# Squares of the RMS norms folded by VectorE before TensorE's column sums, and the order of transposes and value products in the attention rounds, on one core

## What is computed

```
for i in range(4):                                  # layers
    h = rms_norm(x, g[0])
    m = retention(h) | causal pooling(h) | dilated attention(h)   # i mod 3
    x = x + rms_norm(m, g[1])
    x = x + rms_norm(swiglu(rms_norm(x, g[2])), g[3])
rms_norm(x, g) = x * rsqrt(mean(x*x, over the 1024) + eps) * g
attention, per head: o = softmax(q k^T + bias) v, over three dilation groups
```

## Time and profile before

| | us |
|---|---|
| median of 3 runs | 1918.61 |
| lowest, highest | 1913.48, 1918.93 |
| the profiled execution | 1915.92 |
| its span | 1914.1 |

### The profile page before, as it was taken

The page is one execution under the profiler, slowest core; times in us unless marked ns, Lnnn a source line. Parts: engine busy times, 40 slices in busy tenths (PEclk is TensorE's granted clock), DMA queues, the critical chain, the costliest instruction groups (busy, mean ns, idle before and its releaser), DMA issues.

```text
span 1914.1 us, 32457 instructions
## 1 busy us (share of the span) xinstructions
PE 1828.6 (96%) x14108; PEld 1761.3 (92%) x14108; DVE 1039.6 (54%) x1120; ACT 910.9 (48%) x1064; POOL 773.9 (40%) x225
## 2 busy tenths in 40 slices
PE   8999999999979999999999979999999999899997
PEld 7999989999969999888989968999999999899997
DVE  4454555675386654455545463776254455557743
ACT  5555555444454435344444443443455565554443
POOL 4545434555215554321221201355354454455541
PEclk9999989999989999999999988999999999899999
DMA  8766854555435555845455522454667668545552
GB/s 269 260 222 245 296 177 154 186 180 166 129 111 172 181 168 187 238 144 160 140 160 141 159 71 68 131 176 161 209 219 265 225 240 289 187 133 176 176 182 84
DMA packets 306036, 346.33 MB, mean 181 GB/s; under 512 B 7847, under 2 KB 269479, under 8 KB 305887
## 3 DMA queue, kind: packets, MB, share of 16 engines
q1 hardware_dynamic: 257968, 260.36, 43.2%
q10 hardware_dynamic: 47927, 83.90, 12.5%
HBM read 299.66 MB, written 44.82 MB: 180 GB/s over the span
## 4 chain that ended last, share of the span: by engine, by line
PE 82%; DVE 9%; ACT 4%; issue 2%; DMA 1%; ACTq 1%; PEldq 0%; DVEq 0%
PE acc L1485 20%; PE acc L1486 20%; PE acc L1492 20%; PE mix L1625 2%; PE mix L1921 2%; PE mix L1883 1%; PE mix L1547 1%; PE acc L1513 1%; ACT w_hi L433 1%; PE acc L1514 1%; DVE w_lo L925 1%; PE acc L1519 1%; PE mix L1856 1%; PE mix L1637 1%; PE mix L1714 1%
## 5 line engine op out<-in xcount | busy, mean ns | idle before, releaser
L1392 POOL TENSOR_TENSOR w_lo<-raw,w_hi 128x2048 fp32r<-128x2048 f32 (+2 forms) x162 | 690.3, 4266 | 712.0 <-ACT w_hi L433 712.0
L1485 PE MATMUL acc<-g_hi,w_hi 128*128 128x264 f32 x2544 | 638.2, 289 | 8.7 <-DVE gate L1182 2.9
L1486 PE MATMUL acc<-g_lo,w_hi 128*128 128x264 f32 x2544 | 627.4, 284 | 0.0
L433 ACT ACTIVATE w_hi<-raw 128x2048 fp32r<-128x2048 f32 (+3 forms) x260 | 455.7, 1755 | 160.7 <-PE acc L1492 79.1
L925 DVE TENSOR_TENSOR w_lo<-raw,w_hi 128x2048 fp32r<-128x2048 f32 (+2 forms) x98 | 381.1, 3888 | 269.0 <-ACT w_hi L433 269.0
L1485 PEld LDWEIGHTS acc<-g_hi,w_hi 128*128 128x128 f32 x2544 | 478.3, 188 | 17.2 <-issue 12.2
L1486 PEld LDWEIGHTS acc<-g_lo,w_hi 128*128 128x128 f32 x2544 | 480.8, 189 | 1.3
L1492 PE MATMUL acc<-g_hi,w_lo 128*128 128x264 f32 x2544 | 343.8, 285 | 0.6 <-POOL w_lo L1392 0.6
L1492 PEld LDWEIGHTS acc<-g_hi,w_lo 128*128 128x128 f32 x2544 | 325.9, 188 | 2.3 <-POOL w_lo L1392 0.8
L1425 POOL TENSOR_TENSOR h_lo<-hid,h_hi 128x528 fp32r<-128x528 f32 x44 | 59.1, 1343 | 332.9 <-ACT h_hi L707 332.9
L1485 PE MATMUL acc<-h_hi,w_hi 128*128 128x264 f32 x664 | 164.1, 284 | 0.0
(11 more groups left out here) (238 smaller groups left out, 2460.1 us busy)
## 6 DMA issues: line engine op xcount, KB each, us to landing
raw<-in_w_ffn_in_dram SPq DMA_DIRECT2D x88, 1024.0 KB, 5.3
raw<-in_w_in_ret_dram SPq DMA_DIRECT2D x48, 1024.0 KB, 7.0
raw<-in_w_in_attn_dram SPq DMA_DIRECT2D x36, 1024.0 KB, 5.6
st<-in_state_ret_dram ACTq DMA_DIRECT2D x64, 512.0 KB, 6.7
out_dram<-st ACTq DMA_DIRECT2D x64, 512.0 KB, 6.2
raw<-in_w_ffn_out_dram SPq DMA_DIRECT2D x32, 768.0 KB, 4.8
raw<-in_w_ffn_out_dram SPq DMA_DIRECT2D x32, 640.0 KB, 4.9
raw<-in_w_out_ret_dram SPq DMA_DIRECT2D x16, 1024.0 KB, 7.5
```

The costliest lines, as they stand in the source:

```text
L433: A(w_hi[:, u % SPL, 0:size[u]], raw[:, u % RAW, 0:size[u]], ACT.Copy).then_inc(hi_split, 1)
L1392: TT(w_lo[:, u % SPL, 0:size[u]], raw[:, u % RAW, 0:size[u]], w_hi[:, u % SPL, 0:size[u]].bitcast(F32), ALU.subtract).then_inc(lo_by_pool, 1)
L1485: MM(out, wh, x_hi[:, ks[k], :], start=first and k == 0, stop=False)
L1486: MM(out, wh, x_lo[:, ks[k], :], start=False, stop=False)
```

## The change

In `pre_rest` VectorE folds further: after the third pair it adds the fourth (tiles 6 and 7, so it waits for the fourth square), then tile 1 onto tile 0. `pre_stat` is then one matmul instead of four. In `post_evac` VectorE adds tile 1 onto 0 behind L963, waits for the square of tile 6 and adds it too, ahead of the copy of that half; `post_stat` sums tiles 0 and 7, two matmuls instead of four. The pooling layer's sums stay. In attention `turn_probs` of the round of n-1 stands ahead of `values` of the round of n-2. Its wait for the evacuated values goes back one round and covers all its transposes; `values` no longer waits for it; ScalarE's copy to `pT`, which overwrites what those values read, waits for it instead.

```diff
--- before.py
+++ after.py
@@ -791,6 +791,8 @@
                 def turned_out(i):
                     n = 3 * P * (i % 2 + 1)
                     act.wait_ge(pt_done, i + 1)
+                    if i:
+                        act.wait_ge(pv_read, i)
                     A(pT[:, 0:n], mix[:, 0:2, :].rearrange("p b n -> p (b n)")[:, 0:n], ACT.Copy)\
                         .then_inc(pt_ready, 1)
 
@@ -949,7 +951,10 @@
 
                 if sub != POOL_SUB:
                     dve.wait_ge(x_squared, 4 * sub + 3)
-                    TT(sq[:, 0:2, :], sq[:, 0:2, :], sq[:, 4:6, :], ALU.add).then_inc(pre_summed, 1)
+                    link(TT(sq[:, 0:2, :], sq[:, 0:2, :], sq[:, 4:6, :], ALU.add))
+                    dve.wait_ge(x_squared, 4 * sub + 4)
+                    link(TT(sq[:, 0:2, :], sq[:, 0:2, :], sq[:, 6:8, :], ALU.add))
+                    TT(sq[:, 0, :], sq[:, 0, :], sq[:, 1, :], ALU.add).then_inc(pre_summed, 1)
                 if sub == 0:
                     lo(1)
                 lo(where[sub, "in"] + 2)
@@ -960,7 +965,10 @@
 
                 if p == 3:
                     dve.wait_ge(y_squared, 5 * sub + 3)
-                    TT(sq[:, 0:2, :], sq[:, 0:2, :], sq[:, 4:6, :], ALU.add).then_inc(post_summed, 1)
+                    link(TT(sq[:, 0:2, :], sq[:, 0:2, :], sq[:, 4:6, :], ALU.add))
+                    link(TT(sq[:, 0, :], sq[:, 0, :], sq[:, 1, :], ALU.add))
+                    dve.wait_ge(y_squared, 5 * sub + 4)
+                    TT(sq[:, 0, :], sq[:, 0, :], sq[:, 6, :], ALU.add).then_inc(post_summed, 1)
                 pair = pair_at[sub, "out"] + p
                 if p < 3:
                     dve.wait_ge(unit_done, u + 1)
@@ -1548,8 +1556,7 @@
                 ins.then_inc(signal, 1)
 
             def pre_stat(sub):
-                column_sums([(sq[:, 0, :], (pre_summed, sums_at(sub))), (sq[:, 1, :], None),
-                             (sq[:, 6, :], (x_squared, 4 * sub + 4)), (sq[:, 7, :], None)], stat)
+                column_sums([(sq[:, 0, :], (pre_summed, sums_at(sub)))], stat)
 
             def post_stat(sub):
                 if sub == POOL_SUB:
@@ -1560,8 +1567,7 @@
                         ins = TR(mix[0:PREV + DECB, 2 + k // 4, (k % 4) * P:(k % 4 + 1) * P], tail[:, k, :], ident)
                     ins.then_inc(tail_turned, 1)
                     return
-                column_sums([(sq[:, 0, :], (post_summed, sums_at(sub))), (sq[:, 1, :], None),
-                             (sq[:, 6, :], (y_squared, 5 * sub + 4)), (sq[:, 7, :], (y_squared, 5 * sub + 5))], stat)
+                column_sums([(sq[:, 0, :], (post_summed, sums_at(sub))), (sq[:, 7, :], (y_squared, 5 * sub + 5))], stat)
 
             KK = list(range(KD))
 
@@ -1847,8 +1853,6 @@
                 def values(i):
                     quad, hh, c = i // 8, i % 8 // 2, i % 2
                     pe.wait_ge(pt_ready, i + 1)
-                    if i:
-                        pe.wait_ge(pv_read, i)
                     pe.wait_ge(row_evac, 6 * (quad + 1))
                     t = hh // 2
                     blocks = [(g, kb) for g in range(3) for kb in range(c + 1)]
@@ -1862,9 +1866,9 @@
                     pe.wait_ge(p_ready, i + 1)
                     if i:
                         pe.wait_ge(pt_ready, i)
+                    if i > 1:
+                        pe.wait_ge(pv_read, i - 1)
                     for j in range(n):
-                        if j == 4:
-                            pe.wait_ge(pv_read, i)
                         ins = TR(mix[:, j // 4, (j % 4) * P:(j % 4 + 1) * P], sc[i % 2][:, j * P:(j + 1) * P], ident)
                     ins.then_inc(pt_done, 1)
 
@@ -1938,10 +1942,10 @@
                         decode_read(quad - 1, s)
                     if n and (n - 1) % 3:
                         turn_rows(n - 1)
+                    if round_at(n - 1) is not None:
+                        turn_probs(round_at(n - 1))
                     if round_at(n - 2) is not None:
                         values(round_at(n - 2))
-                    if round_at(n - 1) is not None:
-                        turn_probs(round_at(n - 1))
                     if round_at(n) is not None:
                         scores(round_at(n))
                 def out_part(p, ks, last=False):
```

## The result

| | before | after |
|---|---|---|
| median of the executions shown | 1916.30 us (4) | 1929.48 us (4) |
| lowest to highest | 1913.48 to 1918.93 | 1928.67 to 1930.62 |
| profiled execution | 1915.92 us | 1928.67 us |
| its span | 1914.1 us | 1926.9 us |
| mean granted clock of it | 0.978 | 0.968 |

The changed kernel takes 13.2 us more. The forecast was 1924, 7.1 us more, with a range of 1908 to 1934. The sign and the range held. The centre was 5.5 us short. Some parts of the sum hit within tenths and others missed by several us in both directions, so the parts are what follows.

The account below looks back on a forecast made before the run. TensorE, 82% of the chain, was taken as the bound. Ends +11.6, starts +0.2, attention -5.3 and -4.4, clock +5 gave +7.1 us: 1923.0 from the profiled execution, 1925.7 from the median, stated as 1924, range 1908 to 1934.

Parts of the forecast that it names:

- Steps 1 and 2: Column sums: 74 records, not 144, at most 15.5 us gained; ends of subs 1 and 7 gain 0.63 us each.
- Steps 3 to 5: Ends of subs 3 and 5 (+5.6 us), 4 (+3.1), 0 and 6 (+4.2): GpSimd's L1392 blocks VectorE's additions.
- C: Rival: additions issued inside GpSimd's L1392 are not blocked; -15 us, 1902; chance 0.10.
- Steps 6 and 7: Starts of subs 1, 3, 4, 5, 7 about 0.3 us earlier each (-1.5); start of sub 6, reciprocal earlier, -0.6.
- Step 8: Start of sub 0: second new addition caught behind GpSimd's L1392, weight work queued behind it; loss 2.3 us.
- Step 9: Attention, rounds 0 to 23: 9.3 us of evacuation waits go, late scaling in some rounds costs; -5.3 us.
- Step 10: Attention tail: TensorE idle removed, VectorE becomes the limit; rounds 27 and 28 start 2.2 us earlier, the end 4.4.
- Step 11: Seams where TensorE stands still: short half-clock stretches mostly on the cover, 1 us a seam, +5 us.
- B: Rival: blocks come but the clock holds, and attention gives all; 1919 us; chance 0.22.
- D: Rival: attention gives nothing while the folds cost as forecast; 1933 us; chance 0.15.
- A: As forecast: every addition met by L1392 is stretched; centre 1924 us, 1916 to 1932; chance 0.48.
- E: Rival: the change hardly acts, nothing moves; chance 0.05.

Follow-up runs that it names:

- hold: Changed kernel, but GpSimd's last weight remainder waits for VectorE's additions at ends of subs 0, 3, 4, 5, 6; 0.999 of the kernel before.
- psum_add: Changed kernel, but in subs 3 and 5 the square of tile 6 goes to PSUM, where VectorE's last addition reads it; 1.0026 of the kernel before.
- three: Changed kernel without the addition of tile 6 at the ends, so TensorE sums three tiles there; 0.9999 of the kernel before.
- att_only: Kernel before with only the attention part of the change, column sums as before; 0.9967 of the kernel before, 6.3 us faster.

## Why the forecast was right, and where not

- **Steps 1 and 2, records and the free ends.** Right: 74 records, -0.59 twice for -0.63.
- **Steps 3 to 5, the blocked additions.** Right in mechanism, place and size: 3.00 us in subs 3 and 5, 2.97 in sub 4, 4.73 and 4.67 in sub 0; +2.73 and +2.7 at full clock in subs 3 and 5 (forecast 2.8), +1.91 and +2.21 in 0 and 6 (2.1). Shown by hold, psum_add and three. The rival that the folds are not blocked (C) is out. Sub 4: +4.04 with half clock, for 3.1.
- **Steps 6 and 7, the starts.** Right: -0.25 to -0.35 for -0.3, -0.65 for -0.6. The reciprocal does set it.
- **Step 8, start of sub 0.** +2.64 for +2.3. Right: the first new addition got through at 0.71 us, the second was caught for 4.68, and the weight work L927 queued behind it started at 27.93.
- **Step 9, rounds 0 to 23.** The idle time for the evacuation went and the late rounds took 1.37 more each, as forecast; without half clock it would have been -2.37 - 3.0 = -5.4, forecast -5.3. What failed is that the step put no clock behind the two waits it lengthened to 2.8 us. It also took ScalarE's lateness in these rounds as given, though its source is the block of step 3 (L1286 in the earlier trace rows).
- **Step 10, the tail.** Rounds 27 to 30: -2.1 and -3.65 (forecast -2.2 and -3.8). The end was forecast at -4.4 and came at -3.0 in round 31. With the 3.54 us from round 30 to 31 that the full clock gives, 0.74 less than before, it would be -4.4, an estimate: VectorE's chain was right, and the half-clock stretch of 3.4 us took 1.4. Another 1.0 was lost by the start of the out-projection, in a half-clock stretch of 17 us (1153.5 to 1170.6). The kernel before has as much of it there, in two parts (6.8 and 10.2), so that this 1.0 is put down to the clock only by the comparison with the stretches of 20.5 us.
- **Step 11, the clock.** The mechanism was right, the size was not: +5 forecast, 10.4 by places and 12 by the slope. Two things in it failed. It took the lost time as a loss on the work behind the seam, with the L2001 matmuls as cover; but the clock fell while the sums ran, with no cover, 0.95 us in each of subs 3, 4 and 5. And it looked at the seams alone, not at attention, where 5.4 us went.
- **The first projections of sub 4** (+1.71) were in no step. 0.9 of it is a weight tile rounded later, since ScalarE's issue of the cache loads ended 5.76 us later than before in a stretch that was 4.86 later; the rest is half clock from 788.3.
- **Rivals.** B, blocks without clock, gives the structure nearly right by the estimate above, but not the time. By the time alone D (1933) is nearer to the 1929.5 than A's centre (1924); it is out by att_only. C is out by the additions' lengths, E by both.
- **The signs of being wrong.** One of the two, that L1868's waits come back on ScalarE, is at odds, as it is worded, with step 9 and the line ahead of it, which expect two of them at about 2.9 us. They came, at 2.8, as step 9 has it, so this sign decides nothing.
- **The sum.** Of the 5.7 us between +7.1 and +12.8, attention is 5.3 short of its gain, the ends are 2.8 over, the starts 0.3, and the unforeseen rows (+1.7, +1.3, -0.8) make 2.2; the 5 us set aside for the clock stand against them. Most of it is one miss: 10.4 us of clock where 5 were set aside.

## What to carry to other kernels

Before VectorE gets a small job on the path, look at what GpSimd does in that very microsecond: here 0.43 us of VectorE's became 3 to 4.7, and either one wait on the neighbour or one input in PSUM took it away. Leave the last, path-bound part of a reduction with the engine that is there anyway: three tiles instead of two were worth 13 us. And a wait of TensorE is to be priced with the clock that goes with it: a few idle matmuls in it were worth as much as the order of the work (1.5 against 1.4 us a place).

## What the runs showed of the hardware

- The same work ran at another clock from execution to execution. The end of retention in sub 0 stood at the lower level for 17.1 us in the profiled execution of before, for 13.7 in after, for 6.8 in att_only, and was 4.0 us shorter in the last than in the first, though its instructions are the same. Two windows, of before and of att_only (busy us of TensorE, granted clock, DMA share, GB/s):

```profile
264.20:277.80 13.60, 12.92 (x60) 0.50 0.48 158
```

```profile
264.40:271.30 6.90, 6.04 (x29) 0.51 0.90 309
...
271.30:281.50 10.20, 9.01 (x72) 1.00 0.00 0
```

- An addition of VectorE with one input in SBUF and one in PSUM runs at its own length (0.430 us, both times) in the midst of a GpSimd instruction that holds one with two SBUF inputs for 3 us.
- A stretch at half clock cost less than half of its length: 3.4 us of it behind rounds 4 and 20 cost 1.3 to 1.6. The slope over the executions says the same, as an estimate: 0.001 of the mean clock is 3.8 us more at the lower level of a span of 1914, and it went with 1.24 us.
